# Five of six pairs of modulation products of a two-layer mixer block, moved from TensorE to row sums on VectorE

## The reference

```python
silu_c = jax.nn.silu(c)
silu_cc = jax.nn.silu(c_ctx)
for l in range(DEPTH):                    # DEPTH = 2
    last = l == DEPTH - 1
    mod = silu_c @ w_ada[l] + b_ada[l]    # w_ada[l]: 1024 x 6144
    sh1, sc1, gt1, sh2, sc2, gt2 = [m[:, None, :] for m in jnp.split(mod, 6, axis=-1)]
    modc = silu_cc @ w_ada[l] + b_ada[l]
    ...
    h = modulate(rmsnorm(x, g_mix[l]), sh1, sc1)      # h * (1 + scale) + shift
    p = h @ w_in[l]
    x = x + gt1 * latent_mixer(p, ...)                # attention A, attention B, short convolution, gates, w_out
    h2 = modulate(rmsnorm(x, g_ffn[l]), sh2, sc2)
    x = x + gt2 * expert_choice_ffn(h2, ...)          # 16 experts, top-k tokens for each
    if not last:
        ...                                           # the same for the context with modc
```

## Time and profile before

| what | value |
|---|---|
| time, median of 3 runs | 3529.16 us (3526.13 to 3535.64) |
| the profiled execution, its own time | 3529.06 us |
| its span, first to last instruction | 3527.3 us |
| mean granted TensorE clock | 0.979 |
| busy: PE, PEld, DVE, ACT, POOL | 93%, 62%, 35%, 28%, 6% |
| transfers of `w_ada`, 512 KB each | 96, landing in 4.9 us (median) |

### The profile page before, as it was taken

The page is one execution under the profiler, slowest core; times in us unless marked ns, Lnnn a source line. Parts: engine busy times, 40 slices in busy tenths (PEclk is TensorE's granted clock), DMA queues, the critical chain, the costliest instruction groups (busy, mean ns, idle before and its releaser), DMA issues.

```text
span 3527.3 us, 48003 instructions
## 1 busy us (share of the span) xinstructions
PE 3276.5 (93%) x21246; PEld 2201.5 (62%) x21250; DVE 1242.0 (35%) x1821; ACT 1004.1 (28%) x1571; POOL 221.3 (6%) x142
## 2 busy tenths in 40 slices
PE   6999999999699999989999996988879999989998
PEld 4787667888334343467768882332327766858887
DVE  3335642233401011145563333111126444353333
ACT  3623541122210001037343222000022354342223
POOL 0100000121000000001000220000002010020000
PEclk9999999999799999999999998999999999999999
DMA  7540014221899999743102329999983121323331
GB/s 216 149 144 25 1 49 120 66 61 60 323 399 398 390 351 395 299 65 83 39 1 72 96 90 370 421 421 421 421 321 86 34 59 37 96 60 96 101 96 66
DMA packets 385614, 617.00 MB, mean 175 GB/s; under 512 B 99234, under 2 KB 288896, under 8 KB 360704
## 3 DMA queue, kind: packets, MB, share of 16 engines
q1 hardware_dynamic: 378064, 596.50, 47.9%
q0 software_dynamic: 4384, 15.73, 1.3%
q10 hardware_dynamic: 2960, 1.71, 0.2%
HBM read 606.54 MB, written 7.34 MB: 174 GB/s over the span
## 4 chain that ended last, share of the span: by engine, by line
PE 81%; DMA 10%; DVE 4%; ACT 3%; issue 1%; ACTq 0%; POOL 0%; SPq 0%; DVEq 0%
PE ps L592 32%; PE ps L1844 6%; PE ps L2228 5%; PE ps L1083 4%; DMA ring<-in_w_e_up 4%; PE ps L1172 3%; PE ps L1847 3%; PE ps L644 3%; DMA ring<-in_w_e_down 3%; PE ps L1880 3%; PE ps L1133 3%; PE ps L1347 3%; PE ps L1839 2%; PE ps L613 2%; PE ps L1885 2%; PE ps L1876 2%
## 5 line engine op out<-in xcount | busy, mean ns | idle before, releaser
L592 PE MATMUL ps<-xh,wh 128*128 128x512 f32 x1912 | 635.2, 370 | 25.1 <-DVE xl L2074 14.8
L592 PE MATMUL ps<-xh,wl 128*128 128x512 f32 x1912 | 628.3, 367 | 0.0
L592 PE MATMUL ps<-xl,wh 128*128 128x512 f32 x1912 | 627.7, 366 | 0.0
L565 DVE TENSOR_TENSOR wl<-ring,wh 128x1024 fp32r<-128x1024 f32 (+1 forms) x259 | 333.0, 1286 | 443.1 <-ACT wh L556 441.5
L592 PEld LDWEIGHTS ps<-xh,wh 128*128 128x128 f32 x1912 | 329.3, 188 | 106.8 <-issue 25.9
L556 ACT ACTIVATE wh<-ring 128x1024 fp32r<-128x1024 f32 (+1 forms) x259 | 272.0, 1050 | 422.2 <-PE ps L592 162.7
L592 PEld LDWEIGHTS ps<-xh,wl 128*128 128x128 f32 x1912 | 328.8, 188 | 60.3
L592 PEld LDWEIGHTS ps<-xl,wh 128*128 128x128 f32 x1912 | 328.3, 188 | 58.1 <-issue 0.5
L1844 PE MATMUL ps<-ring,arena 128*32 128x512 f32 x1344 | 176.8, 598 | 0.9 <-ACT arena L1592 0.9
L1839 PE MATMUL ps<-ring,arena 128*64 128x512 f32 x704 | 162.7, 604 | 12.5 <-DMA ring<-in_w_e_up 8.0
L1094 DVE TENSOR_REDUCE sm<-ps 128x2 f32<-128x1536 f32 (+3 forms) x96 | 142.3, 1482 | 45.4 <-PE ps L1083 45.0
(11 more groups left out here) (277 smaller groups left out, 4444.4 us busy)
## 6 DMA issues: line engine op xcount, KB each, us to landing
ring<-in_w_e_gate SPq DMA_DIRECT2D x87, 1024.0 KB, 20.4
ring<-in_w_e_up SPq DMA_DIRECT2D x85, 1024.0 KB, 19.7
ring<-in_w_e_down SPq DMA_DIRECT2D x85, 1024.0 KB, 21.3
ring<-in_w_in SPq DMA_DIRECT2D x112, 512.0 KB, 4.0
ring<-in_w_ada SPq DMA_DIRECT2D x96, 512.0 KB, 4.9
arena<-in_w_e_up SPq DMA_DIRECT2D x43, 1024.0 KB, 17.4
arena<-in_w_e_down SPq DMA_DIRECT2D x43, 1024.0 KB, 20.7
arena<-in_w_e_gate SPq DMA_DIRECT2D x41, 1024.0 KB, 20.0
```

Source lines behind the costliest of these rows:

```text
L565: e.tensor_tensor(in_heads(X, u, m.WL[:, o:o + many]), heads_of(X, u, halves.aps[s], many), in_heads(X, u, m.WH[:, o:o + many].bitcast(F32 ...
L592: i = e.matmul(ps[0:M, a:b], w[:, k, 0:M], h[:, k, a:b], start=k == 0 and p == 0, stop=k == 7 and p == 2)
```

## The change

Pair 0 stays as it was. For the others, `w_ada` is read in quarters of a pair: g = 0 to 19 counts the quarters of pairs 1 to 5, each 1024 rows by 512 columns in four parts of 256 rows (one piece of the ring each). `dve_mod_part` multiplies each block of 128 rows by the per-partition scalar silu(c) and adds it to `ACC[0]`, and for pairs 1 to 3 the same with silu(c_ctx) into `ACC[1]`; pairs 4 and 5 use one vector. After the last part the 512 columns are turned in 32x32 blocks into `TR` and summed over each 32 (`RS`). That leaves four groups of partitions, which `pe_fold` adds by four small products with the constant `fold`, now 32 columns wide; `dve_fold` adds the bias. One part stands on VectorE at the end of each of the first eight convolution units (g 0 and 1), two at the end of each gate step t < 20 of layer 0 (g 2 to 11) and t < 16 of layer 1 (g 12 to 19). The tiles, the copies on ScalarE and the transposes of these pairs go, and so do their transfers at the old places.

```diff
+        MODS = [(pair, q) for pair in range(1, 6) for q in range(4)]
+        vectors = lambda g: (0, 1) if MODS[g][0] < 4 else (0,)
+        def mods_beside_conv(j):
+            return [(j // 4, j % 4)] if j < 8 else []
+        def mods_beside_gate(l, t):
+            i = t // 2
+            return [((2, 12)[l] + i, 2 * (t % 2) + c) for c in (0, 1)] if i < (10, 8)[l] else []
+        def folds_beside_gate(l, t):
+            return [MODS[g][0] for g in ((2, 12)[l] + t // 2 - 2,) if t % 2 == 0 and 0 <= t // 2 - 2 < (10, 8)[l] and MODS[g][1] == 3]
...
+            def mods(parts):
+                for g, c in parts:
+                    X.raw(("mods", g, c), *mod_quarter(g, c), d_md, "mod", g, 2 * c + 1, vectors(g)[-1])
...
+        def dve_mod_part(e, X, g, c):
+            s, srcs, many, kind, what, arrived = X.pieces[X.plain["mods", g, c]]
+            e.wait_ge(*arrived)
+            for k in (2 * c, 2 * c + 1):
+                src = halves.aps[s][:, 512 * (k % 2):512 * (k % 2) + 512]
+                for w in vectors(g):
+                    if k == 0:
+                        if g:
+                            e.wait_ge(*d_md.at("turn", g - 1, w if w in vectors(g - 1) else 0))
+                        e.tensor_scalar(ACC[w], src, csv[:, 0, w:w + 1], None, ALU.mult).then_inc(*d_md.up("mod", g, k, w))
+                        continue
+                    e.wait_ge(*d_md.at("mod", g, k - 1, w))
+                    e.scalar_tensor_tensor(out=ACC[w], in0=src, scalar=csv[:, k, w:w + 1], in1=ACC[w], op0=ALU.mult,
+                                           op1=ALU.add).then_inc(*d_md.up("mod", g, k, w))
+            if c < 3:
+                return
+            pair, q = MODS[g]
+            if q == 0 and pair > 2:
+                e.wait_ge(*p_modt.at("mod", pair - 2))
+            for w in vectors(g):
+                e.wait_ge(*d_md.at("mod", g, KD - 1, w))
+                if w or g:
+                    e.wait_ge(*(d_md.at("sum", g, 0) if w else d_md.at("sum", g - 1, vectors(g - 1)[-1])))
+                e.transpose(TR, ACC[w]).then_inc(*d_md.up("turn", g, w))
+                e.wait_ge(*d_md.at("turn", g, w))
+                e.tensor_reduce(RS[:, pair % 2, q, w], TR.rearrange("p (b i) -> p b i", i=32), AX, ALU.add).then_inc(*d_md.up("sum", g, w))
...
             for br in range(3):
                 for d in range(KD):
                     t = 8 * br + d
-                    if l == 0 and t == 8:
-                        pe_modt(e, 3)
                     pe_linear3(e, X, ("g", br, d), 128, T, (X.key, "g", t), g_sg.at(X.key, t))
-                    if l == 0 and t < 8:
-                        pe_mod(e, 48 + 2 * t)
+                    for pair in folds_beside_gate(l, t):
+                        pe_fold(e, pair)
...
                     dve_low(e, X, X.unit["g", br, d] + 1)
-                    if l == 0 and t == 8:
-                        dve_mod(e, 3)
+                    for pair in folds_beside_gate(l, t - 1):
+                        dve_fold(e, pair)
                     if d % 2:
...
                         weigh(br, d)
+                    for g, part in mods_beside_gate(l, t):
+                        dve_mod_part(e, X, g, part)
...
-            mods(*range(68, 80))
...
-            mods(*range(80, 88))
...
-            if l == 0:
-                pe_modt(e, 4)
...
-            mods(*range(88, 96))
-            if l == 0:
-                pe_modt(e, 5)
```

More of the change, by code:

```diff
@@ L667, in pe_mod, with act_mod @@
             i.then_inc(*p_mod.up("mod", m))
[L668 to L677, removed]
+            if m == 15:
+                bank.back("mod")
+        def act_mod(e):
+            e.wait_ge(*p_mod.at("mod", 15))
+            e.activation(MR0, bank.of["mod"][:, 0:512], ACT.Copy).then_inc(*c_mod.up("mod"))
@@ new lines, in pe_modt, with dve_mod @@
+        def pe_modt(e):
+            ps, when = bank.take("modt", d_mod.at("mod", 0, 1))
+            for w in when:
+                e.wait_ge(*w)
+            e.wait_ge(*c_mod.at("mod"))
+            for c in range(4):
+                i = e.transpose(ps[:, 128 * c:128 * c + 128], MR0[:, 128 * c:128 * c + 128], ident)
+            i.then_inc(*p_modt.up("mod", 0))
+        def dve_mod(e):
+            e.wait_ge(*p_modt.at("mod", 0))
+            pv = bank.of["modt"][:, 0:512].rearrange("p (n h g w) -> p n g h w", n=2, h=2, g=4)
+            for nb in (0, 1):
+                o = modv[:, 0, 8 * nb:8 * nb + 8, :].rearrange("p (g h) w -> p g h w", h=2)
+                b = PT[:, 32 + 8 * nb:40 + 8 * nb].rearrange("p (g h) -> p g h", h=2)
+                e.tensor_tensor(o, pv[:, nb, :, :, 0:2], b.unsqueeze(3).broadcast_to([128, 4, 2, 2]),
+                                ALU.add).then_inc(*d_mod.up("mod", 0, nb))
+            dve_gain(e, 0)
@@ L678, in pe_modt, with pe_fold @@
+        def pe_fold(e, pair):
             ps, when = bank.take(("modt", pair), d_mod.at("mod", pair, 1))
@@ L680, in pe_modt @@
                 e.wait_ge(*w)
-            e.wait_ge(*c_mod.at("mod", pair))
-            for c in range(4):
-                i = e.transpose(ps[:, 128 * c:128 * c + 128], MR(pair)[:, 128 * c:128 * c + 128], ident)
+            g = MODS.index((pair, 3))
+            many = len(vectors(g))
+            e.wait_ge(*d_md.at("sum", g, many - 1))
+            sums = RS[:, pair % 2, :, 0:many].rearrange("p q w (k g) -> p g q w k", g=4)
+            for g in range(4):
+                i = e.matmul(ps[32 * g:32 * g + 32, 0:16 * many].rearrange("p (q w k) -> p q w k", q=4, w=many), K("fold"), sums[:, g],
+                             start=True, stop=True)
@@ L684, in pe_modt, with dve_fold @@
             i.then_inc(*p_modt.up("mod", pair))
-        def dve_mod(e, pair):
+        def dve_fold(e, pair):
             l, n2 = pair // 3, pair % 3
+            many = len(vectors(MODS.index((pair, 3))))
             e.wait_ge(*p_modt.at("mod", pair))
[L689 to L695, removed]
-            if n2 != 1:
[L697 to L701, removed]
@@ L705, in act_square @@
+            ps = bank.of["modt", pair][:, 0:16 * many].rearrange("p (q w k) -> p q k w", q=4, w=many)
+            o = modv[:, l, 16 * n2:16 * n2 + 16, 0:many].rearrange("p (q k) w -> p q k w", q=4)
+            b = PT[:, 32 + 48 * l + 16 * n2:48 + 48 * l + 16 * n2].rearrange("p (q k) -> p q k", q=4)
+            e.tensor_tensor(o, ps, b.unsqueeze(3).broadcast_to([128, 4, 4, many]), ALU.add).then_inc(*d_mod.up("mod", pair, 1))
+            if n2 != 1:
+                dve_gain(e, pair, many)
         def act_square(e, stage, k, src, T, bufs, total=None, seen=lambda t: t):
@@ L793, in act_start @@
             act_rstd(e, "n0", KD, T0, D)
[L794 removed]
+            act_mod(e)
         def dve_start(e):
```

91 lines of the change are left out of this document (31 added, 60 removed).

## The result

The changed kernel takes 3560.94 us (3557.44 to 3562.43, four runs) against 3527.64 us (3524.62 to 3535.64, four runs) of the kernel before in the same comparison: ratio 1.0093, 95% interval 1.0081 to 1.0105. It is slower by 33.3 us; forecast was 3562.6, that is +33.5. The profiled execution took 3561.9 us with a span of 3559.9.

A forecast was written before the change was run, and what follows sets the result against it. TensorE, busy 93% of the span, was taken as the bound, stalling when VectorE's low halves come late. Terms -15.7 + 36.3 + 23.4 + 6.0 + 1.2 - 17.7 = +33.5 on 3529.06 gave 3562.6 us, range 3541 to 3588.

The forecast's parts named there:

- Projections, -15.7: Layer 0's projections: removed tiles and turns give -18.2 us, a stall at unit j = 3 with its restart adds 2.5.
- the clock charge for j = 3: Convolution unit j = 3, layer 0: half of the 1.7 us clock loss, 0.85, charged for its 2.2 us stall.
- Gates of layer 0: Layer 0's gate loop: stalls at odd steps cost 53.3 us, 17.0 of old cost goes, +36.3 before half clock charges.
- Gates of layer 1: Layer 1's gate loop: late low halves at odd t stall TensorE, +23.4 us before half clock charges.
- The clock: TensorE behind stalls: 1.7 us charged to each over 3.5 us, half to seven of 2.2 to 2.3, these +6.0.
- Choice, -17.7: Layer 0's choice: earlier logits -11.2, norm's total -1.0, index product -1.6 and gather -3.9 us.
- the part for the gather, -3.9: Layer 0's choice: gather falls from 8.36 to 4.49 us as expert loads go out during the norm.
- The two rules beside the sum: VectorE, outside the total: 0.59 us per 512 columns by the skill's table; ports shared with GpSimd go to whoever starts first.
- Room on VectorE (3477): Rival, gates: odd step under 6.0 us in layer 0, 3.4 in layer 1, no late low half; -52 us; chance 0.09.
- Stalls half as long: Rival, gates: GpSimd's additions kept out (-14), no clock loss (-21); about 3529 to 3541 us; chance 0.10.
- A choice that gains little: Rival, layer 0's choice: gather waits for stores behind early expert loads, -17.7 shrinks to about -6; 3574 us; chance 0.10.
- No piece of `w_ada` was late: Answers the rival on gates' late w_ada pieces: about 5 us more at ten odd steps, 3600 or above; chance 0.05.

The follow-up runs named there:

- short additions: Changed kernel with GpSimd's additions in the merge cut to 8 columns, the rest of the merged sum left out: 3535.49 us, ratio 1.0019 to the kernel before.
- late loads: Changed kernel with the first seven expert loads of layer 0 held until the first expert's indices are ready: 3565.7 us, ratio 1.0106 to the kernel before.
- one vector: Changed kernel with the context's modulation of pairs 1 to 3 left out, taking the latent tokens' values: 3516.05 us, ratio 0.9966 to the kernel before.
- filler products: Changed kernel with TensorE multiplying a constant during its stalls, into the bank the next product overwrites: 3537.77 us, ratio 1.0029 to the kernel before.
- the move of the parts: Changed kernel with all parts moved up on VectorE, right behind the low half that opens their step: 3478.0 us, ratio 0.9860 to the kernel before.

## Why the prediction was right, point by point

The mechanism is the one that was forecast: the low half is late, by about the length worked out. That the total agrees to 0.2 us (33.3 against 33.5) is luck: the stages are off by up to 3.7 us, in both directions, and one of them, +3.5 in the experts, has nothing to do with the change.

*Projections, -15.7.* At their end the chain of the changed kernel is 15.8 us ahead of before's (280.91 against 296.68), with the clock charge for j = 3 spent in it. Ahead of the gates it is 17.0: the other 1.2 us fall in the attention, which the change doesn't touch and which takes 196.8 to 199.4 us from trace to trace. The stall at j = 3 is there: the run of 33.93 us ends at 210.24, the next unit's 8.48 at 218.72, and TensorE goes on at 220.85, 2.1 us of stall against the 2.2 worked out.

*Gates of layer 0.* The working of a step held to a tenth of a microsecond: an odd step takes 8.19 us where 8.2 stood, the run from branch product to odd gate 10.44 where 10.5 stood, GpSimd adds 1.6 where 1.66 stood. The turn, which no row of before showed, takes 0.70 us against 0.73. The cycles of branch 0 are 27.34 us and those of branches 1 and 2 29.1 to 30.6 (but for t = 7 and 15 with their splits). In sum +35.7 against +39.4. The ten stalls are 37.5 us where the terms have 39.2, as each is 0.1 to 0.2 shorter; the clock took 12.9 us where 14.5 were charged. The restart is 0.23 (8.56 against 8.33), charged at 0.25.

*Gates of layer 1.* Too low by 3.1 us. Its terms add up to 23.65, where 23.4 stands. The branch 0 cycle is 18.08, +1.42 as forecast. GpSimd costs 0.92 us and not 1.1. The stalls are 17.8 us where the terms have 18.3. But all three stalls of about 2 us in branch 1 lowered the clock (7.3 instead of 5.69 us), where I charged half, and those at t = 7 and 15 cost 2.65 and 2.34 us instead of 1.7.

*The clock.* The weakest term, and it came out by compensation: of seven stalls of about 2 us in all, five lowered it, where I charged half; of the stalls over 3.5 us, all charged, the one at t = 9 did not. Nor is it a coin toss. Counted over the changed kernel and the runs with short additions, late loads and one vector, stalls of 2.0 to 2.1 us lowered the clock in 4 of 15 cases in the gates of layer 0, and in 9 of 9 in those of layer 1. Stalls of 1.2 us never did (15 cases in the same four traces, all in layer 1). What sets the two layers apart within 2 us stays open; the total of the charges, 21 us, was near the 23 that the filler products took away.

*Choice, -17.7.* Measured -18.9; the part for the gather, -3.9, measured -4.2, and late loads gave it back. Of the rest, the start of the logits' product gained 11.2 us where 12.2 were forecast, and from there to the gather it is 3.4 instead of 1.6: without the tiles ahead of it the logits' product itself takes 1.48 us and not 2.75, at a granted clock of 1.00 and not 0.50. No term had that.

*The two rules beside the sum.* By the table in the Trainium skill, "VectorE: DVE Perf Modes", section on the TRN2 errata, the odd step would be 7.1 us, as the prediction estimated; the trace has 8.19, so that table is too low here. The same section of the Trainium skill gives 691 ns for a float32 addition of 512 columns; the sum and the turn, which are other operations, take as long in the trace (0.69 and 0.70 us), while a multiply-add takes 0.76. The Trainium skill, "SBUF — State Buffer", section on the two separate sides, says that VectorE and GpSimd share ports and whoever holds them keeps the other out; the trace agrees (1.68 against 0.76 us, and with GpSimd's additions cut 0.76 throughout).

*The rivals.* Room on VectorE (3477) was wrong for the kernel as written, but it is near what the move of the parts gives: 3478.0. (That they agree to 1 us is in part chance: the gates gained 13.6 us and not 17.0, the choice 20.0 and not 17.7.) The work fits; its place did not. Stalls half as long fell with the 3.72 us of four multiply-adds beside GpSimd's addition and with the clock of 0.59 and 0.57. A choice that gains little fell with the gather's 4.13 us. No piece of `w_ada` was late: in the gates of the changed kernel no engine waits for a transfer.

## What to carry to other kernels

An engine that is 35% busy has room only where it is idle by its own order. Before work is put into such a gap, find what the engine produces next for the bottleneck, and put the new work right behind that, not ahead of it: the same instructions, moved by some lines, made 83 us of difference here. Count the run from the releasing event to the needed result against what the bottleneck has left to do; it is a threshold: here, half of the work had almost no cost in layer 0.

## What the runs showed of the hardware that was not expected

Whether TensorE's clock drops behind an idle stretch of 2 to 2.5 us can't be told from its length. At one place it differs from execution to execution: with the same stall of 2.1 us at t = 1, the changed kernel lost 1.6 us and the run with late loads 0.15, and at the end of the first expert's stage four of eight traces have the drop. From place to place the share differs too: 4 of 15 stalls in layer 0, 9 of 9 in layer 1. A few small products in the stall kept the clock at 1.00, at under 0.1 us a stall in layer 0.

Between two multiply-adds that wait for each other GpSimd gets in after the first one, and only once for each of its own instructions: in branch 1 of layer 1 it is the second of four that takes 1.68 us, at all four odd steps, and the others keep 0.76.
